# Projection units woven into the index scores and dealt out anew over HGRN; attention blocks in the order 4, 5, 6, 7, 3, 2, 1, 0; a shorter search step; one level mask on ScalarE

## The chip, the cores and the metric

The kernel is one launch on one NeuronCore of one Trainium2 chip. The metric is the device time in microseconds. Its engines run side by side, each in its own order, and wait for each other on semaphores: TensorE (PE, matmuls and transposes into the eight banks of PSUM), VectorE (DVE), ScalarE (ACT), GpSimd (POOL) and SyncE (SP, which issues the weight loads).

## The reference, cut to what matters

One layer of a decoder is computed for a prompt of 1024 tokens and for 8 single tokens ("samples") with a paged cache of 8192 past positions each: an FFN, a mixer, a second FFN, each with a residual and a LayerNorm. All is float32. Only the mixer is touched. It projects the hidden state into everything that the two halves of the mixer need, and then:

```python
# attention half: an indexer scores all keys, the best 256 are attended
logits = einsum('bqhd,bld->bqhl', qi, kidx) * (64 ** -0.5)
score  = einsum('bqh,bqhl->bql', wi * (8 ** -0.5), relu(logits))   # masked causally
_, idx = top_k(score, 256)
o_attn = softmax(q . k[idx]) @ v[idx]                              # 8 heads, 2 kv heads
# HGRN2 half: gated linear recurrence, 8 heads of 64x64 state
f = lb + (1 - lb) * sigmoid(rf);  k = 1 - f
S_t = diag(f_t) S_{t-1} + k_t i_t^T;  o_t = S_t^T q_t
o_r = rmsnorm(o) * norm_g * silu(rg)
m = concat([o_attn, o_r]) @ w_out
```

For prompt positions below 256 every causal key is selected, so the first two blocks of 128 queries (0 and 1) need no search.

## The kernel before, in words

The mixer runs in stages. The prompt is cut into 8 blocks of 128 queries; block b has 128(b+1) keys, so blocks 2 to 7 have widths 384 to 1024. Projections are cut into **units** (`UNITS`): eight matmuls over the model dimension into one PSUM bank, then one ScalarE copy out of it. A long unit ("f", line 528) gives 128 features for 344 tokens, a short one ("t", line 533) 256 or 72 features for 128 tokens. `unit_done` counts finished units, `unit_out` copied ones; unit u uses bank u % 3 and waits until unit u - 3 has been copied.

1. **Units 0 to N1 - 1**: index queries, keys, values, index keys and weights.
2. **Index scores** (PE lines 559 to 576, ACT 918 to 925, DVE 1107 to 1118): for blocks 2 to 7 and each pair of heads TensorE forms both heads' logits, the head with the first 64 rows of the array and the second with the others. ScalarE writes ReLU of one head into one of two buffers, VectorE adds it, times the query's weight, to the block's score. A head's logits fill two banks; a pair uses banks 0 to 3 or 4 to 7 in turn and waits for the ReLUs of the pair before the last. Before all this TensorE waits for `sn_ready`, the score of each sample's new token (five small VectorE operations, lines 1087 to 1092).
3. **32 rounds**: each searches one bit of the 256th largest score of every query on VectorE and ScalarE (32 rounds for 32 bits of a float), while TensorE transposes gathered cache keys of the samples (line 584), runs **one unit** (q, the gates of t = 0, ri), and forms the samples' index logits (line 593).
4. **HGRN** for t = 0 to 3, two heads each, in the level form of a scan: for levels lv = 0 to 7, VectorE forms the operands of a level (`level`, 1272 to 1277), TensorE its products in two halves (`level_products`, 652), and the entries that belong to this level are kept from PSUM in `AT`: by VectorE with a mask for levels 0 to 6 minus one (`mask`, 1286 and 1290: levels 0 to 5), by ScalarE with block copies for levels 6 and 7 (`block_copy`, 952). Units are listed beside the levels (`BESIDE`) and after levels 5 and 6 (`AFTER`). Where a level has two or more, the first runs before the second `count` of the level, else the only one runs after it. Woven in, twice per level, is one step of the samples' own search: `sample_bit` (1160, 1131 to 1133), `sample_compare` (1155, 1156) on VectorE, `count` (607) on TensorE. In t = 1 and 2, VectorE also turns the scores of blocks 7 and 6 into masks (`keep_top`, two parts, in levels 2 and 3). In t = 3 the samples' selection runs instead (`select_a` to `select_d`); its buffers lie over ring slots 0 and 1, so `select_a` waits until all units are out.
5. **Attention** in 64 steps (block, head), blocks 7 down to 0: logits (723), masked maximum on VectorE (1375), exponent on ScalarE (977), transposes (736), copy (987), times values (749). From step 32 on it runs two steps ahead instead of one. `keep_top` of the block two below stands after heads 4 and 5. A sample state update (1393 to 1400) stands after head 6 of the second to fifth block.
6. The output projection (858), LayerNorm, second FFN.

SyncE loads weight slabs into four ring slots in one order. The slab of w_out in slot 2 (`mix(14)`) waits until all six masks are made, since masks are built in that slot.

`link(...)` makes VectorE wait for the end of an instruction before its next one. `NBITS` and `ROUNDS` are 32, `FIRST_TOPK` 2, `H` 8, `BLK` 8, `DT` 8, `TW` 344.

Of the kernel before, what the change touches and what calls it, by code (L numbers as in the profile page):

```python
# [9 lines left out]
def build_decoder_step(nc, I, O):  # L10
# [34 lines left out]
    with ctx:  # L45
# [283 lines left out]
        UNITS += gate_units(0, 0) + gate_units(0, 1) + row_units("ri", 0) + ri1[:5]  # L329
# [24 lines left out]
        assert N2 - N1 == ROUNDS  # L354
# [3 lines left out]

        def steps():

            return [(b, h) for b in range(BLK - 1, -1, -1) for h in range(H)]
# [150 lines left out]
        def pe_mixer(pe, cols, mean, var):  # L512
# [3 lines left out]
            def unit(u):  # L516
                kind, name, m, a, x, _ = UNITS[u]
                pe.wait_ge(ring_in[m % 4], mix_reach[m])
                if kind == "f":
                    pe.wait_ge(ln_done, x + 1)  # L520
                else:
                    pe.wait_ge(ln_done, 2 if x < 5 else 3)
                if u >= 3:
                    pe.wait_ge(unit_out, u - 2)
                for k in range(DT):
                    if kind == "f":
                        w = RING[:, m % 4, :].rearrange("p (k c) -> p k c", c=SLAB)
                        last = M(PS[:, u % 3, 0:TW], w[:, k, P * a:P * a + P], ACTS[:, k, cols(x)],  # L528
                                 start=k == 0, stop=k == DT - 1)
                    else:  # L530
                        rows = P if x < BLK else NB
                        w = RING[:, m % 4, 0:DT * a].rearrange("p (k c) -> p k c", c=a)
                        last = M(PS[0:rows, u % 3, 0:a], ACTS[:, k, P * x:P * x + rows], w[:, k, :],  # L533
                                 start=k == 0, stop=k == DT - 1)
                last.then_inc(unit_done, 1)
# [1758 lines left out]
```

## Time and profile before

| | us |
|---|---|
| median of 3 runs (lowest, highest) | 2722.03 (2721.08, 2722.7) |
| the profiled execution's own time | 2723.82 |
| its span | 2722.1 |
| TensorE busy | 2587.1 (95%) |
| VectorE busy | 1528.5 (56%) |
| ScalarE busy | 664.2 (24%) |
| GpSimd busy | 536.2 (20%) |

Busy times are of single engines in one profiled execution. The chain that ended last gives 80% of the span to PE and 13% to DVE. A matmul's end is modelled, so a busy TensorE is not one at its peak. The granted TensorE clock of a stretch is given as a share of full speed.

### The profile page before, as it was taken

The page shows a single profiled execution, that of the slowest core. Times are in us where ns is not written, and L with a number is a line of the kernel's source. Part 1 is how long each engine was busy: PE and PEld are TensorE (multiplying, and loading weights), DVE is VectorE, ACT ScalarE, POOL GpSimd, SP SyncE. Part 2 cuts the span into 40 slices and gives each one's busy share as a digit, 9 for nine tenths or more (in the row PEclk, how much of TensorE's full clock was granted, in tenths as well). Part 3 has the DMA queues.
Part 4 walks back from the last instruction along what each step waited for, and adds up shares of the span by engine and source line. Part 5 has one row for each costly group of instructions (what it writes and reads, how often), then busy time and mean ns, then how long its engine had stood idle before and what let it go on. Part 6 is the DMA issues. An engine that isn't in the chain of part 4 may idle for free.

```text
span 2722.1 us, 42485 instructions
## 1 busy us (share of the span) xinstructions
PE 2587.1 (95%) x16989; PEld 2360.9 (87%) x16989; DVE 1528.5 (56%) x3030; ACT 664.2 (24%) x1519; POOL 536.2 (20%) x518
## 2 busy tenths in 40 slices
PE   8999999999999979998998789999999999999997
PEld 8989999999998747897766667768999999999997
DVE  5544465546542187797778866425654465546543
ACT  1110122012201255662221156502220022002212
POOL 5230233023301011110000012313330233023300
PEclk9999999999999999999999799999999999999999
DMA  7455246534642113320010012103464346434642
GB/s 187 124 146 137 75 125 170 137 81 124 167 134 77 48 36 93 102 86 1 2 32 1 2 50 66 28 1 93 126 171 129 86 124 167 128 93 124 167 117 90
DMA packets 456371, 261.67 MB, mean 96 GB/s; under 512 B 21720, under 2 KB 448840, under 8 KB 456176
## 3 DMA queue, kind: packets, MB, share of 16 engines
q1 hardware_dynamic: 448736, 238.48, 33.3%
q0 software_dynamic: 7440, 20.49, 2.6%
q8 instruction: 136, 2.23, 0.3%
q14 instruction: 59, 0.48, 0.1%
HBM read 252.12 MB, written 6.81 MB: 95 GB/s over the span
## 4 chain that ended last, share of the span: by engine, by line
PE 80%; DVE 13%; issue 4%; ACT 1%; SPq 1%; DMA 1%; DVEq 0%; ACTq 0%
PE ps L1681 33%; PE ps L1747 20%; PE ps L528 8%; PE ps L533 5%; PE ps L858 4%; PE ps L593 2%; PE ps L652 1%; PE ps L749 1%; DVE down_weights L1118 1%; PE ps L723 1%; PE ps L584 1%; DVE aux L1290 1%; PE ps L736 1%; DMA weight_ring<-ffn_wu 1%; DVE weight_ring L1375 1%
## 5 line engine op out<-in xcount | busy, mean ns | idle before, releaser
L1681 PE MATMUL ps<-aux,big 128*128 128x172 f32 x2112 | 333.5, 311 | 14.7 <-ACT big L1882 14.6
L2062 DVE TENSOR_TENSOR weight_ring<-ps,big 128x172 f32<-128x172 f32 x396 | 123.7, 331 | 386.3 <-ACT big L1882 350.7
L1681 PEld LDWEIGHTS ps<-aux,big 128*128 128x128 f32 x2112 | 315.8, 191 | 19.9 <-ACT big L1882 17.9
L1681 PE MATMUL ps<-acts,weight_ring 128*128 128x172 f32 x2112 | 322.9, 311 | 9.7 <-DMA weight_ring<-ffn_wg 5.3
L1681 PE MATMUL ps<-weight_ring 128*128 128x172 f32 x2112 | 329.5, 309 | 0.0
L1681 PEld LDWEIGHTS ps<-acts,weight_ring 128*128 128x128 f32 x2112 | 314.0, 192 | 11.6 <-DMA weight_ring<-ffn_wg 5.6
L1681 PEld LDWEIGHTS ps<-weight_ring 128*128 128x128 f32 x2112 | 313.8, 190 | 0.0
L1747 PE MATMUL ps<-big 128*128 128x172 f32 x1584 | 238.8, 309 | 0.0
L1747 PEld LDWEIGHTS ps<-big 128*128 128x128 f32 x1584 | 233.1, 190 | 0.0
L528 PE MATMUL ps<-acts,weight_ring 128*128 128x344 f32 x768 | 230.8, 456 | 0.0
L2222 POOL TENSOR_TENSOR big<-weight_ring 128x512 f32<-128x512 f32 x66 | 83.7, 1269 | 666.3 <-PE ps L1681 619.8
L1882 ACT ACTIVATE big<-ps 128x172 f32<-128x172 f32 x396 | 117.6, 309 | 390.5 <-PE ps L1681 390.5
L528 PEld LDWEIGHTS ps<-acts,weight_ring 128*128 128x128 f32 x768 | 144.3, 191 | 71.8 <-issue 2.0
L1886 ACT ACTIVATE weight_ring<-weight_ring 128x172 f32<-128x172 f32 x198 | 68.0, 343 | 487.1 <-DVE weight_ring L2062 487.1
L533 PE MATMUL ps<-weight_ring,acts 128*128 128x256 f32 (+3 forms) x864 | 179.1, 362 | 0.0
L2123 DVE SCALAR_TENSOR_TENSOR acts<-acts,ps 128x172 f32<-128x172 f32 x96 | 31.7, 331 | 251.4 <-PE ps L1747 251.4
L1681 PE MATMUL ps<-acts,big 128*128 128x172 f32 x1056 | 165.6, 310 | 0.0
L533 PEld LDWEIGHTS ps<-weight_ring,acts 128*128 128x128 f32 (+1 forms) x864 | 141.9, 179 | 26.6 <-issue 1.3
L1747 PE MATMUL ps<-big,weight_ring 128*128 128x172 f32 x1056 | 159.9, 309 | 0.0
L1747 PE MATMUL ps<-big,down_weights 128*128 128x172 f32 x1056 | 159.9, 309 | 0.0
L1681 PEld LDWEIGHTS ps<-acts,big 128*128 128x128 f32 x1056 | 158.1, 191 | 0.0
L1747 PEld LDWEIGHTS ps<-big,down_weights 128*128 128x128 f32 x1056 | 155.5, 190 | 0.0
(344 smaller groups left out, 3676.7 us busy)
## 6 DMA issues: line engine op xcount, KB each, us to landing
weight_ring<-ffn_wg SPq DMA_DIRECT2D x132, 512.0 KB, 5.2
weight_ring<-ffn_wu SPq DMA_DIRECT2D x132, 512.0 KB, 7.1
down_weights<-ffn_wd SPq DMA_DIRECT2D x24, 1408.0 KB, 11.6
weight_ring<-ffn_wd SPq DMA_DIRECT2D x24, 1408.0 KB, 9.5
weight_ring<-w_in SPq DMA_DIRECT2D x9, 1024.0 KB, 5.2
weight_ring<-w_in SPq DMA_DIRECT2D x8, 512.0 KB, 5.2
weight_ring<-w_out SPq DMA_DIRECT2D x4, 1024.0 KB, 6.2
big<-x_prompt SPq DMA_DIRECT2D x7, 512.0 KB, 6.1
```

Source lines behind the costliest of these rows:

```text
L528: last = M(PS[:, u % 3, 0:TW], w[:, k, P * a:P * a + P], ACTS[:, k, cols(x)], start=k == 0, stop=k == DT - 1)
L533: last = M(PS[0:rows, u % 3, 0:a], ACTS[:, k, P * x:P * x + rows], w[:, k, :], start=k == 0, stop=k == DT - 1)
L584: last = T(PS[:, 3 + j // 4, P * (j % 4):P * (j % 4) + P], KX[:, r % 4, P * j:P * j + P], IDENT[:, :])
L593: last = M(PS[:, 5 + r % 2, 32 * j:32 * j + 32], KXT[:, r % 2, P * j:P * j + P], QB[:, :, :, 2 * gp:2 * gp + 2], start=True, stop=True)
L858: last = M(PS[:, Y_BANK[y], 0:TW], w[:, k, P * (d % 2):P * (d % 2) + P], src, start=k == 0, stop=k == DT - 1)
L1681: last = M(PS[:, 3 * m + bank, 0:QW], lhs[:, i, :], rhs[:, i, :], start=begin and i == 0, stop=end and i == KH - 1, skip_group_check=True)
L1747: last = M(PS[:, x + bank, 0:QW], lhs[:, i, :], rhs[:, i, :], start=begin and i == 0, stop=end and i == LAST, skip_group_check=True)
L1882: A(ST[:, m, c, :], PS[:, 3 * m, 0:QW], ACT.Copy).then_inc(cp_done, 1)
L1886: A(CG[:, i, :], CG[:, i, :], ACT.Silu).then_inc(sl_done, 1)
L2062: V.tensor_tensor((CG, CU)[m][:, (out, i)[m], :], PS[:, 3 * m + bank, 0:QW], ST[:, m, part, :], ALU.add)\
L2123: V.scalar_tensor_tensor(a, a, 2 * ALPHA, PS[:, x + bank, 0:QW], ALU.mult, ALU.add).then_inc(zr_done, 1)
L2222: G.tensor_tensor(s1, a21, a22, ALU.add).then_inc(su_done[0], 1)
```

## The change

Four long units (q) are taken out of the rounds: one stands before the index scores, in place of the wait for the new tokens' scores, three are cut into single k steps, one after each pair of heads. To free banks 0 and 1 for them, scores use banks 2 to 7 as three slots instead of four, with another wait. All nine units of ri, second half, then lie in the rounds, and the rest is dealt out anew over HGRN. Level 5's mask goes to ScalarE. The attention order becomes 4, 5, 6, 7, 3, 2, 1, 0, with the masks one block ahead and only block 4's within HGRN. The samples' search step is rewritten.

```diff
+        WOVEN = 4
+        def unit_bank(u):
+            return (u - N1) % 2 if N1 <= u < N1 + WOVEN else u % 3
+        def bank_free(u):
+            return u if u == N1 + WOVEN else u - 1 if N1 + 2 <= u < N1 + WOVEN else u - 2
...
-        UNITS += gate_units(0, 0) + gate_units(0, 1) + row_units("ri", 0) + ri1[:5]
+        UNITS += gate_units(0, 0) + gate_units(0, 1) + row_units("ri", 0) + ri1
...
-        for beside, spread in (([g1[0], *rg0[:2], g1[1], *rg0[2:4], g1[2], *rg0[4:6]], (2, 1, 2, 1, 2, 1, 0, 0)),
-                               ([g2[0], *rg0[6:8], g2[1], rg0[8], ri1[5], g2[2], *ri1[6:]], (2, 1, 2, 1, 2, 2, 0, 0)),
-                               ([g3[0], *rg1[:2], g3[1], *rg1[2:4], g3[2], *rg1[4:6]], (2, 1, 2, 1, 2, 1, 0, 0)),
-                               (rg1[6:], (2, 1, 0, 0, 0, 0, 0, 0))):
+        for beside, spread in (([g1[0], *rg0[:2], g1[1], *rg0[2:4], g1[2], rg0[4]], (2, 1, 2, 1, 1, 1, 0, 0)),
+                               ([g2[0], *rg0[5:7], g2[1], *rg0[7:9], g2[2], rg1[0]], (2, 1, 2, 1, 1, 1, 0, 0)),
+                               ([g3[0], rg1[1], g3[1], rg1[2], g3[2], rg1[3]], (1, 1, 1, 1, 1, 1, 0, 0)),
+                               (rg1[4:], (2, 2, 1, 0, 0, 0, 0, 0))):
...
+        ORDER = (4, 5, 6, 7, 3, 2, 1, 0)
...
+            unit(N1)
-            pe.wait_ge(k3_ready, 9)
-            pe.wait_ge(sn_ready, 1)
+            pe.wait_ge(k3_ready, 10)
...
-                if pr >= 2:
-                    pe.wait_ge(ix_relu, 2 * pr - 2)
+                if pr:
+                    pe.wait_ge(ix_relu, 2 * pr - 1)
...
-                        last = M(PS[:, 4 * (pr % 2) + 2 * e + c // 512, 0:min(512, n - c)], QIT[rows, hp, P * b:P * b + P],
+                        last = M(PS[:, 2 + 2 * ((2 * pr + e) % 3) + c // 512, 0:min(512, n - c)], QIT[rows, hp, P * b:P * b + P],
...
+                unit(N1 + 1 + pr // DT, pr % DT, pr % DT + 1)
...
-                unit(N1 + r)
+                unit(N1 + WOVEN + r)
...
-                    if lv >= 6:
+                    if lv >= 5:
                         block_copy(t, lv)
...
+            def new_scores():
+                dve.wait_ge(k3_ready, 10)
+                link(V.tensor_tensor(QIPROD, QITOK, KIW[0:NB, 8:9, 0:HD].to_broadcast([NB, H, HD]), ALU.mult))
...
                 if h == 0:
+                    if i == H:
+                        new_scores()
...
                 link(V.tensor_tensor(DCMP, SDEC, cand[:, 6:10].unsqueeze(2).to_broadcast([P, 4, PAGE + 1]), ALU.is_ge))
+                V.tensor_scalar(CAND[:, 6:10], CAND[:, 6:10], BITS[:, k + 1:k + 2], None, ALU.bitwise_xor)
                 V.tensor_reduce(DCNT, DCMP, AX.X, ALU.add).then_inc(dcmp_done, 1)
...
-                next_bit(slice(6, 10), k)
+                link(V.scalar_tensor_tensor(CAND[:, 6:10], REJ[:, 6:10], BITS[:, k:k + 1], CAND[:, 6:10],
+                                            ALU.bitwise_and, ALU.bitwise_xor))
...
-                    if lv < 7:
+                    if lv < 6:
                         mask(t, lv - 1)
                     sample_slot(t, lv, 1)
-                    if 0 < t < 3 and lv in (2, 3):
-                        keep_top(BLK - t, lv - 2)
+                    if t == 2 and lv in (2, 3):
+                        keep_top(ORDER[0], lv - 2)
...
-                if i % H in (4, 5) and STEPS[i][0] - 2 >= FIRST_TOPK:
-                    keep_top(STEPS[i][0] - 2, i % H - 4)
+                if i % H in (4, 5) and i // H < 7 and ORDER[i // H + 1] >= FIRST_TOPK:
+                    keep_top(ORDER[i // H + 1], i % H - 4)
...
-                        if t == 1:
+                        if t == 2:
                             mix(14)
```

The three woven units run to the last pair of heads, eight k steps each; ScalarE copies each out after 16 ReLUs. At the start of the kernel one of the small mask-building steps on VectorE moves to an earlier place. The waits on counts of masks and copies are renumbered to match.

## Rows read from the trace of the kernel before

**Rows 1.** Windows, all engines: us, busy us of each engine (x instructions), PEclk, DMA.

```profile
966.82:1016.60 49.78, 36.84 (x161) 14.62 (x161) 42.65 (x47) 36.22 (x48) 8.74 (x16) 0.94 0.15 27
1238.28:1313.10 74.82, 70.12 (x439) 55.85 (x439) 58.16 (x107) 11.59 (x18) 0.95 (x1) 0.95 0.00 1
1324.39:1407.47 83.08, 75.18 (x454) 57.10 (x455) 67.63 (x120) 14.71 (x23) 1.50 (x1) 0.92 0.10 27
1418.69:1497.11 78.42, 69.01 (x436) 53.95 (x437) 64.79 (x114) 15.64 (x23) 1.50 (x1) 0.96 0.00 1
1508.32:1528.57 20.25, 19.20 (x160) 15.39 (x160) 16.53 (x23) 5.20 (x8) 0.00 (x0) 0.92 0.01 2
1577.26:1746.75 169.49, 155.77 (x1144) 122.76 (x1145) 98.98 (x270) 101.45 (x216) 52.11 (x54) 0.97 0.22 57
```

**Rows 2.** Lines by form, index scores: busy us, mean ns, idle before.

```profile
L1118 DVE SCALAR_TENSOR_TENSOR down_weights<-big,aux,down_weights 128x1024 f32<-128x1024 f32 x7 | 9.0, 1284 | 0.8 <-ACT big L925 0.2
...
L1118 DVE SCALAR_TENSOR_TENSOR down_weights<-big,aux,down_weights 128x384 f32<-128x384 f32 x7 | 4.3, 618 | 0.8
...
L925 ACT ACTIVATE big<-ps 128x1024 f32<-128x1024 f32 x8 | 8.2, 1024 | 2.5 <-DVE down_weights L1118 2.5
...
L925 ACT ACTIVATE big<-ps 128x384 f32<-128x384 f32 x8 | 3.8, 491 | 7.6 <-PE ps L572 7.2 <-DVE down_weights L1118 0.4
```

**Rows 3.** Timeline, start of the index scores: start us, us, engine, line, operation [idle before].

```profile
966.82 6.76 PE L572 MATMUL ps<-big 64*128 64x384 f32 x20 [2.80 <-issue]
```

**Rows 4.** Timeline, attention, a pair of 1024-wide logits and its reader.

```profile
1592.88 1.99 PE L723 MATMUL ps<-big 64*128 64x512 f32 x8
...
1594.89 1.23 DVE L1375 CUSTOM_DVE_ANT_0 weight_ring<-ps,down_weights 128x1024 f32<-128x1024 f32 x1 [3.96 <-PE ps L723]
```

**Rows 5.** Chain that ended last, a long and a short round: start us, us.

```profile
1041.10 4.63 PE ps L528 x16
...
1161.83 3.46 PE ps L533 x16
```

**Rows 6.** Timeline of VectorE, HGRN t = 0.

```profile
1236.35 0.17 DVE L1251 COPY down_weights<-big 128x8 f32<-128x8 f32 x1
...
1236.43 0.69 DVE L1252 TENSOR_SCALAR big<-big 128x1032 f32<-128x1032 f32 x1
...
1263.26 0.16 DVE L1160 TENSOR_SCALAR rejected<-ps 128x4 int32<-128x4 f32 x1 [2.13 <-PE ps L607]
...
1264.18 0.70 DVE L1155 TENSOR_TENSOR big<-down_weights,candidate 128x516 bf16<-128x516 f32 x1
...
1265.52 2.47 DVE L1290 COPY_PREDICATED aux<-level_masks,ps 128x1024 f32<-128x1024 uint8 x2
...
1267.89 0.14 DVE L1160 TENSOR_SCALAR rejected<-ps 128x4 int32<-128x4 f32 x1
...
1270.13 0.68 DVE L1272 TENSOR_TENSOR weight_ring<-big,weight_ring 128x512 f32<-128x512 f32 x1
...
1272.78 0.16 DVE L1160 TENSOR_SCALAR rejected<-ps 128x4 int32<-128x4 f32 x1
```

**Rows 7.** Timeline of TensorE, HGRN t = 0.

```profile
1276.47 3.65 PE L652 MATMUL ps<-weight_ring 64*128 64x128 f32 x32 [0.90 <-DVE aux L1290]
...
1303.55 9.50 PE L528 MATMUL ps<-acts,weight_ring 128*128 128x344 f32 x32
```

**Rows 8.** Timeline of ScalarE, level-6 block copies of t = 0.

```profile
1302.01 1.65 ACT L952 ACTIVATE aux<-ps 32x256 f32<-32x256 f32 x4 [5.46 <-PE ps L652]
```

**Rows 9.** Windows of VectorE over keep_top: 1024 first, 640 first, 1024 second.

```profile
1344.29:1348.91 4.62, 4.48 (x6) 1.00 0.02 4
1625.44:1628.66 3.22, 3.08 (x6) 1.00 0.14 41
...
1358.43:1361.79 3.36, 3.26 (x4) 1.00 0.00 0
```

**Rows 10.** Timeline of TensorE, attention, logits behind the 640-wide mask.

```profile
1630.00 1.77 PE L723 MATMUL ps<-big 64*128 64x512 f32 x8 [1.04 <-DVE small L1377]
```

More of the change, by code:

```diff
@@ L353, in build_decoder_step @@
         ROUNDS = 32
-        assert N2 - N1 == ROUNDS
+        assert N2 - N1 - WOVEN == ROUNDS
         DEC_SLOTS = [(t, lv, e) for t in range(3) for lv in range(2, 8) for e in range(2) if lv < 7 or e == 0][:NBITS]
+        ORDER = (4, 5, 6, 7, 3, 2, 1, 0)
+        MASKED_AT = {b: n + 1 for n, b in enumerate(b for b in ORDER if b >= FIRST_TOPK)}
         def steps():
-            return [(b, h) for b in range(BLK - 1, -1, -1) for h in range(H)]
+            return [(b, h) for b in ORDER for h in range(H)]
         STEPS = steps()
@@ L514, in pe_mixer, with unit @@
             loaded = [0]
-            def unit(u):
+            def unit(u, first=0, end=DT):
                 kind, name, m, a, x, _ = UNITS[u]
[L518 to L525, printed above, removed]
+                if first == 0:
+                    pe.wait_ge(ring_in[m % 4], mix_reach[m])
+                    pe.wait_ge(ln_done, x + 1 if kind == "f" else 2 if x < 5 else 3)
+                    if u >= 3:
+                        pe.wait_ge(unit_out, bank_free(u))
+                for k in range(first, end):
                     if kind == "f":
                         w = RING[:, m % 4, :].rearrange("p (k c) -> p k c", c=SLAB)
-                        last = M(PS[:, u % 3, 0:TW], w[:, k, P * a:P * a + P], ACTS[:, k, cols(x)],
+                        last = M(PS[:, unit_bank(u), 0:TW], w[:, k, P * a:P * a + P], ACTS[:, k, cols(x)],
                                  start=k == 0, stop=k == DT - 1)
@@ L532, in unit @@
                         w = RING[:, m % 4, 0:DT * a].rearrange("p (k c) -> p k c", c=a)
-                        last = M(PS[0:rows, u % 3, 0:a], ACTS[:, k, P * x:P * x + rows], w[:, k, :],
+                        last = M(PS[0:rows, unit_bank(u), 0:a], ACTS[:, k, P * x:P * x + rows], w[:, k, :],
                                  start=k == 0, stop=k == DT - 1)
-                last.then_inc(unit_done, 1)
+                if end == DT:
+                    last.then_inc(unit_done, 1)
             def turn_heads(b):
@@ L640, in level_products @@
                 for half in range(2):
-                    if 1 <= lv <= 6:
-                        pe.wait_ge(h_at, 12 * t + 2 * (lv - 1) + half + 1)
-                    elif lv == 7:
-                        pe.wait_ge(h_ax, 4 * t + half + 1)
+                    if 1 <= lv <= 5:
+                        pe.wait_ge(h_at, 10 * t + 2 * (lv - 1) + half + 1)
+                    elif lv >= 6:
+                        pe.wait_ge(h_ax, 6 * t + 2 * (lv - 6) + half + 1)
                     elif t and half:
@@ L684, in pe_mixer @@
                 last.then_inc(h_kt_mm, 1)
-                pe.wait_ge(h_at, 12 * (t + 1))
-                pe.wait_ge(h_ax, 4 * (t + 1))
+                pe.wait_ge(h_at, 10 * (t + 1))
+                pe.wait_ge(h_ax, 6 * (t + 1))
                 def out(hd, c):
@@ L758, in turn_gated @@
             def turn_gated(bi):
-                b = BLK - 1 - bi
+                b = ORDER[bi]
                 if bi < 7:
@@ L882, in unit @@
                 width = TW if kind == "f" else a
-                src = PS[0:rows, u % 3, 0:width]
+                src = PS[0:rows, unit_bank(u), 0:width]
                 cols = slice(TW * x, TW * x + TW)
@@ L917, in act_mixer @@
             A(WIS[0:NB, BLK, :], KIW[0:NB, BLK, HD:HD + H], ACT.Copy, scale=H ** -0.5).then_inc(wis_ready, 1)
+            unit(N1)
             for i in range(6 * H):
@@ L922, in act_mixer @@
                     act.wait_ge(ix_acc, i - 1)
-                k0 = 4 * (i // 2 % 2) + 2 * (i % 2)
+                k0 = 2 + 2 * (i % 3)
                 src = PS[:, k0:k0 + 2, :].rearrange("p u c -> p (u c)")[:, 0:n]
                 A(RELU[:, i % 2, 0:n], src, ACT.Relu, scale=KSCALE).then_inc(ix_relu, 1)
+                if i % 16 == 15:
+                    unit(N1 + 1 + i // 16)
             def keys_out(r):
@@ L941, in act_mixer @@
                 pass_counts(r)
-                unit(N1 + r)
+                unit(N1 + WOVEN + r)
             def block_copy(t, lv):
@@ L989, in out_rows @@
             def out_rows(bi):
-                b = BLK - 1 - bi
+                b = ORDER[bi]
                 act.wait_ge(at_ott, bi + 1)
@@ L1288, in mask @@
                         m = LEVELS[:, lv - 1, :].unsqueeze(1).unsqueeze(1).to_broadcast([P, 2, 4, P])
-                        dve.wait_ge(h_at, 12 * t + 2 * (lv - 1) + half + 1)
+                        dve.wait_ge(h_at, 10 * t + 2 * (lv - 1) + half + 1)
                         V.copy_predicated(at, m, ps).then_inc(h_at, 1)
@@ L2147, in ffn @@
                         if ff == 0 and g == 0:
-                            if 1 <= j <= 7:
-                                dve_consts(dve, V, link, j - 1)
+                            if j == 1:
+                                dve_consts(dve, V, link, 0)
+                            if 1 <= j <= 6:
+                                dve_consts(dve, V, link, j)
                             if 1 <= j <= 6:
```

19 lines of the change are left out of this document (9 added, 10 removed).

## The prediction

> **What bounds the kernel now.** I read the stages first (stretches cut at matmul starts), then in each stage the order of instructions, and there which wait ends last. TensorE is busy almost everywhere, but not for one reason. In the index scores [rows 1] it is busy 36.8 of 49.8 us: VectorE, 42.7 busy, sets the pace, and ScalarE (36.2) must refill a two-deep buffer. In the search rounds TensorE runs without a gap. In HGRN, units t = 0, 1, 2 take 74.8, 83.1 and 78.4 us from the first to the eighth group of level products, TensorE busy 70.1, 75.2 and 69.0 [rows 1]: it waits for VectorE in the middle levels and VectorE waits for it at the rest. Attention has 155.8 busy of 169.5. Nothing in the two FFNs or the output projection is touched, so only these stages count.
>
> **1. Four projection units into the index scores, and the waits there.** One unit (eight k steps, 4.63 us [rows 5]) now stands ahead of the scores, in place of the 2.80 us that TensorE idled for the new token's score [rows 3]. The idle began at 964.0; the unit ends near 968.6, so the first score pair starts 1.8 us later than 966.82. What follows is the part against the change. Before, a pair wrote into four slots and waited for the ReLU of the pair before the last one; now there are three slots and the wait is for the first ReLU of the *previous* pair. That closes a ring: pair, its first ReLU, next pair. At 1024 keys the pair needs 2.01 us until a waiting engine can start (1592.88 to 1594.89, same matmuls [rows 4]), ReLU 1.02 [rows 2], and 0.06 taken for TensorE's restart (an estimate; the reader in [rows 4] started 0.02 after the modelled end): 3.09 us. VectorE needs 2 x 1.39 = 2.78 for the two heads (1.284, and 0.8 idle in seven [rows 2]). At 384 keys: a matmul column costs 4630/8/344 = 1.68 ns, so 2.01 - 640 x 0.00168 = 0.94, with ReLU 0.49 and 0.06 it is 1.49, against 2 x 0.73 = 1.46. Linear between, the mean ring is 2.29 us; 24 pairs give 55.0, and the last ReLU 1.0: 56.0 where 49.8 stand. Sum: 1.8 + 56.0 - 49.8 = **+8.0**. The k step of 0.58 us per pair hides behind the ReLU (at 384 keys, 0.49, it just doesn't). The new token's score, moved behind the first block (some 2 us on VectorE, part of the 2.80 that TensorE waited for it [rows 3]), falls into VectorE's new slack. Ends: +3 if the ring doesn't bind (start 1.8, the moved score 2.0, less a first pair that is no longer at the low clock), +11 if it binds and each k step adds 0.13.
> A page of the Trainium skill, "Perfetto Trace Analysis" (Optimization Strategy), says that the same gap repeating on the engine that should be busy can mean too little PSUM for the next tile. By that rule a slot taken from the scores costs, as the ring says; before's rows show no such gap on VectorE.
>
> **2. Rounds.** Each round is gapless on TensorE, and unit forms differ: 4.63 against 3.46 us [rows 5]. The 32 rounds held 18 long units and 14 short, now 14 and 18: 4 x 1.17 = **-4.7**. Should VectorE be the tighter one in a short round, the gain is less: 3 at the lower end, an estimate.
>
> **3. HGRN.** Edits with one answer: fewer units beside the levels, the level-5 mask to ScalarE, the top-k masks out of t = 1, a short search step. Prices on VectorE [rows 6]: search step 0.92 (1263.26 to 1264.18), compare 1.34, mask 2.37, level operands 2.65 (1270.13 to 1272.78). The step loses two operations of about 0.26 and 0.20 (and + xor become one, taken at 0.26) and its last xor stands unlinked in the compare; the nearest row is a small operation that lets the next start after 0.08 (1236.35 to 1236.43 [rows 6]). New pair of step and compare: 0.46 + 1.42 = 1.88 for 2.26, 0.38 less. Bounds: 0.20 (xor costs 0.26) to 0.46.
> The Trainium skill, "VectorE: DVE Perf Modes" (The DRAIN you can't avoid), says the next operation doesn't start until the pipe is empty, whatever the semaphores. By it the unlinked xor costs full price and the step saves 0.20; the sum would be 2 us less. The 0.08 row speaks for the larger saving.
> Level by level with these prices, TensorE's units 4.73 and 3.55 from start to start, products 2.0, two more units in a row 9.50 [rows 7]:
> t = 0. Nothing moves until the third products. Then masks 2, 3 come 0.4 and 1.2 us earlier. In level 4 the lone long unit now stands *behind* the count, so VectorE no longer waits for it: mask 4 starts 4.8 us earlier. From there TensorE is the bound: short unit, long, products, two long; the level-5 mask on ScalarE (eight small copies, at most 0.41 each by the wider ones [rows 8], 3.3 us) is hidden behind 8.3 us of units. Eighth products at 1307.6 instead of 1313.1: -5.5.
> t = 1. Also loses the 1024-wide mask, 4.62 and 3.36 us [rows 9], and one unit more from level 5. Same ladder: 68.7 from first to eighth products where 83.1 stand: -14.4.
> t = 2. Units (1,1,1,1,1,1) instead of (2,1,2,1,2,1), and a 640-wide mask (3.22 [rows 9], its second part in the same proportion 2.35) for the 896-wide one (between the two, about 4.15 and 3.0). TensorE idles 2.7 us at level 3, VectorE's work sets levels 2 to 5, then units again: 68.2 for 78.4: -10.2.
> t = 3. Five short units instead of three, in levels 0, 1, 2. The sample selection waits until all units have left the banks it reuses. Before, it started 20.25 us after the first products [rows 1]; now products 3.6, two units 7.1, products 2.0, two units 7.1, products 2.0, one unit and its copy 4.0 give 25.8: +5.6. Later its chain is VectorE's without a gap, and loses the mask: -2.4. Together +3.2.
> These sum to -26.9. Against it stands the clock. After idling TensorE runs a product group in 3.65 us instead of 2.06 (at 1276.47, with 0.90 idle right ahead [rows 7]). With fewer units there is about one more such group in each of t = 0, 1, 2, and half of its 1.6 us reaches the path: +2.4. HGRN: **-24.5**, bounds -29 and -15.
>
> **4. Attention in the order 4, 5, 6, 7, 3, ...** The first block is 640 wide instead of 1024: its logits, maximum and exponent, all serial at the start, shrink by 384 columns at 3.36 ns (TensorE, half clock), 1.04 and 0.83 ns ((1284 - 618)/640 and (1024 - 491)/640 [rows 2]): 1.3, 0.4 and 0.3, and a wait two heads later by an estimated 0.6: -2.6. But the masks now prepared are 768, 896, 1024, 512 and 384 wide, in blocks of width 640, 768, 896, 1024 and 512. Before, the 640 mask in the 896 block held the next logits back by 1.04 us [rows 10]. A 1024 mask there puts 4.62 for 3.22: 1.4 more, and the second part (3.36 for 2.35) delays the next wait, behind the sample state, by 1.0. The 768 block with an 896 mask pays the same 2.4; the first block 0.4 net (its second wait has no sample state ahead); block 7 wins 0.9; block 3, which had no mask, pays 1.2. Sum of stalls +5.5, attention **+2.9**, bounds -1 and +9. The w_out load that waits for the last mask comes one block later and still over 30 us ahead of its use: nothing.
>
> **Sum.** +8.0 - 4.7 - 24.5 + 2.9 = -18.3. The profiled execution took 2723.8 (span 2722.1 and 1.7 around it), the runs' median is 2722.0; the difference is applied to the median: 2703.7 us.
>
> **Rivals.**
> A, the ring doesn't bind: semaphore latency overlaps the pair's tail, or the pair is faster than the attention row. Index scores +3, all else the same: 2698.7. For it: with slots four deep no row shows the ring. Against: each of its terms is a row. Chance 0.20.
> B, small blocks can't hide big masks: the steps after a mask queue behind each other, so that each of the three wide masks stalls TensorE by its full second part too (2.7, 3.0, 3.4, less the 1.0 counted): +8 in attention: 2712. For it: the blocks are narrower where the masks are wider. Against: the 1.04 [rows 10] was a third of its mask. Chance 0.15.
> C, slower: the clock of HGRN. If TensorE, with its filler thinned, stays at 1.2 GHz through levels 2 to 5 of t = 0, 1, 2, four product groups (1.6 each), two long (4.7) and two short units (3.5) per t grow by 22.8 us, of which some 8 fall into waits: 45 in three, net +27: 2749. It decides from 6 us per t on. For it: the selection part of t = 3 and the group at 1276.47 ran so. Against: granted clock was 0.92 to 0.96 in t = 0, 1, 2 [rows 1], and a unit right behind each slow group ran at full speed. Chance 0.05.
> The Trainium skill, "TensorE: Matmul & The Clock Gate" (HAM oscillation), warns of this: matmul bursts split by waits run at half clock again and again. The selection part of t = 3 agrees; the rest, at 0.92 and above, doesn't so far.
>
> **How the numbers follow.** Forecast 0.60, A 0.20, B 0.15, C 0.05. Forecast's own range: HGRN and attention bounds combined, 2695 to 2712. The range reaches to A less 7 and B plus 4: 2692 to 2716; C lies outside. What a measurement tells from no change is 0.2%, 5.4 us, so up to 2716.6 is faster: faster 0.93, within 0.02, slower 0.05.
>
> **What would show it.** Index scores: 56 us between first score pair and first key transpose, TensorE waiting on ScalarE's ReLU in each pair, VectorE with gaps of 0.3 at 1024 keys (right), or VectorE gapless (A). Rounds: 14 at 7.24 and 18 at 6.07. First to eighth products: 69.3, 68.7, 68.2 us plus slow groups; selection 25.8 after t = 3's first products. Attention: 172 us with stalls ahead of the logits at the fifth head of blocks 4, 5, 6. Wrong if the ladders miss by over 5 us in one t, or if a granted clock below 0.9 appears there.

## The result, and the profile after

The changed kernel takes 2701.62 us, median of 4 runs (2697.87 to 2704.78), against 2722.36 before on the same chip: ratio 0.9926, 95% interval 0.9912 to 0.994. A second series gave 2700.54 (8 runs, 2698.4 to 2717.56) against 2722.31: 0.9931, interval 0.9913 to 0.9949. The forecast of 2703.7 lies 2 us off, but that is partly luck: the stages show four errors, one of them of 10 us, that cancel in part and leave 5. The profiled execution took 2700.48 us, its span is 2698.8 where 2722.1 stood: 23.3 less, where the sum said 18.3.

Stages are cut at the start of their first TensorE instruction, in us:

| stage | before | after | difference | forecast |
|---|---|---|---|---|
| first FFN | 856.33 | 846.38 | -9.95 | 0 |
| units up to the one ahead of the scores | 107.1 | 107.1 | 0 | 0 |
| index scores, with the start and the unit ahead | 53.2 | 63.0 | +9.8 | +8.0 |
| rounds | 221.68 | 215.23 | -6.45 | -4.7 |
| HGRN | 338.98 | 314.65 | -24.3 | -24.5 |
| attention | 169.49 | 177.17 | +7.7 | +2.9 |
| output projection, second FFN | 975.35 | 975.32 | 0 | 0 |

The windows of the profile after, columns as in [rows 1]: scores, rounds, and the three HGRN parts t = 0, 1, 2 from first to eighth products, then t = 3 up to attention, attention, and its first 10 us.

```profile
958.64:1016.43 57.79, 53.00 (x210) 20.57 (x209) 44.01 (x52) 35.48 (x52) 7.72 (x14) 1.00 0.12 24
1016.43:1231.66 215.23, 211.32 (x1281) 177.73 (x1281) 188.20 (x524) 134.90 (x258) 29.45 (x30) 0.99 0.30 94
...
1231.66:1302.35 70.69, 68.21 (x422) 53.45 (x422) 53.30 (x96) 13.34 (x25) 0.95 (x1) 0.92 0.00 1
1313.65:1383.07 69.42, 66.33 (x423) 50.47 (x423) 54.50 (x99) 17.38 (x30) 1.50 (x1) 0.95 0.06 17
1394.29:1462.79 68.50, 62.29 (x389) 47.49 (x390) 58.07 (x102) 16.62 (x28) 1.50 (x1) 0.90 0.01 1
1474.00:1546.31 72.31, 53.28 (x477) 46.19 (x477) 58.85 (x125) 16.09 (x30) 1.84 (x3) 0.81 0.01 2
1546.31:1723.48 177.17, 160.50 (x1144) 126.06 (x1145) 108.40 (x278) 101.22 (x216) 52.15 (x54) 0.94 0.21 55
1546.31:1556.31 10.00, 7.97 (x30) 5.13 (x31) 6.33 (x18) 3.69 (x7) 3.06 (x3) 0.50 0.73 209
```

In [rows 1] the same stages had TensorE busy 36.84, 70.12, 75.18, 69.01 and 155.77. Attention is the stage to look at: its length grew by 7.7, but TensorE's idle time only from 13.7 to 16.7 (length less busy). The other 4.7 us are the same work done slower, at a granted clock of 0.94 for 0.97.

**Index scores.** The timeline of TensorE in the changed kernel, at 512 and at 1024 keys (L581 the pair, L536 the woven k step):

```profile
968.02 0.85 PE L536 MATMUL ps<-acts,weight_ring 128*128 128x344 f32 x2
970.00 1.13 PE L581 MATMUL ps<-big 64*128 64x512 f32 x4 [1.14 <-ACT big L936]
...
1006.23 1.99 PE L581 MATMUL ps<-big 64*128 64x512 f32 x8 [0.33 <-ACT big L936]
1008.15 0.85 PE L536 MATMUL ps<-acts,weight_ring 128*128 128x344 f32 x2
1009.32 1.99 PE L581 MATMUL ps<-big 64*128 64x512 f32 x8 [0.33 <-ACT big L936]
```

From pair to pair it is 3.09 us at 1024 keys, as forecast, and TensorE waits 0.33 for ScalarE's ReLU each time. Ahead of 970.00 it waits 1.14 longer: there VectorE forms the new tokens' scores, which the forecast let fall into slack.

**First FFN.** What the forecast never looked at. SyncE's load queue (SPq; ffn_wd is the down-projection's weights, ffn_wg and ffn_wu the up-projections') and TensorE in the kernel before:

```profile
163.48 3.71 SPq L1560 DMA_DIRECT2D down_weights<-ffn_wd  x2
167.23 6.60 SPq L1543 DMA_DIRECT2D weight_ring<-ffn_wg  x2
173.87 3.68 SPq L1543 DMA_DIRECT2D weight_ring<-ffn_wu  x2
...
179.55 2.66 PE L1681 MATMUL ps<-acts,weight_ring 128*128 128x172 f32 x8 [5.33 <-DMA weight_ring<-ffn_wg]
183.16 5.92 PE L1681 MATMUL ps<-acts,weight_ring 128*128 128x172 f32 x24 [0.94 <-DMA weight_ring<-ffn_wu]
```

And in the changed kernel, where TensorE has no stall at that place:

```profile
147.24 0.16 DVE L1071 TENSOR_TENSOR lower_bound<-lower_bound 128x4 f32<-128x4 f32 x1
...
147.69 3.73 SPq L1580 DMA_DIRECT2D down_weights<-ffn_wd  x2
157.04 1.13 SPq L1563 DMA_DIRECT2D weight_ring<-ffn_wg  x2
158.22 4.78 SPq L1563 DMA_DIRECT2D weight_ring<-ffn_wu  x2
```

The first down-projection load waits, on SyncE, for `lb_diff`: a VectorE operation that ends the last of the small mask-building steps. The change moved six of these steps, not one, as the section on the change has it: steps 1 to 6 each stand one pair of features earlier, the last one at the sixth instead of the seventh. The load starts 15.8 us earlier, and so do the up-projection loads that queue behind it.

### The profile page after: what moved, and what is told of

Read it like the earlier page. It is cut to its first block, busy times and chain, and to the rows that moved or that the text cites. A ratio compares the mean times of both kernels' runs of the same rounds, so it can differ in the third digit from the quotient of the medians.

```text
span 2698.8 us, 42468 instructions
## 1 busy us (share of the span) xinstructions
PE 2592.4 (96%) x16989; PEld 2357.3 (87%) x16989; DVE 1510.3 (56%) x2990; ACT 670.5 (25%) x1552; POOL 536.1 (20%) x518
## 4 chain that ended last, share of the span: by engine, by line
PE 83%; DVE 11%; issue 3%; ACT 2%; SPq 1%; DMA 0%; DVEq 0%; ACTq 0%
PE ps L1701 33%; PE ps L1767 20%; PE ps L536 8%; PE ps L541 6%; PE ps L868 4%; PE ps L603 2%; PE ps L759 2%; PE ps L662 1%; PE ps L733 1%; PE ps L581 1%; PE ps L594 1%; PE ps L746 1%; DVE aux L1310 1%; DVE weight_ring L1395 1%; SPq L1563 1%
## 5 line engine op out<-in xcount | busy, mean ns | idle before, releaser
L536 PE MATMUL ps<-acts,weight_ring 128*128 128x344 f32 x768 | 240.8, 465 | 0.0
L536 PEld LDWEIGHTS ps<-acts,weight_ring 128*128 128x128 f32 x768 | 145.1, 195 | 80.7 <-issue 16.4
```

What stands on the lines that cost most here:

```text
L536: last = M(PS[:, unit_bank(u), 0:TW], w[:, k, P * a:P * a + P], ACTS[:, k, cols(x)], start=k == 0, stop=k == DT - 1)
```

## Experiments

Medians are of runs beside runs of the kernel before on the same chip, unless a stage is named; stage lengths come from the profile of each kernel.

**1 and 2. The load that waits for a mask-building step.** The same edit put into the kernel before, and taken out of the changed one:

```diff
-                            if 1 <= j <= 7:
-                                dve_consts(dve, V, link, j - 1)
+                            if j == 1:
+                                dve_consts(dve, V, link, 0)
+                            if 1 <= j <= 6:
+                                dve_consts(dve, V, link, j)
```

> The kernel before, with only the order of the small mask-building steps in the first FFN taken from the changed kernel: step 6, which ends in the difference of the lower bounds that the first down-projection load waits for, stands behind the sixth pair of features instead of the seventh. Theory (SyncE's in-order queue stood at that load, and the loads of the up weights queued behind it came too late): the load is issued near 147.7 us instead of 163.5, TensorE's stall of 5.33 us at 179.55 and the slow matmuls behind it are gone, the first mixer unit starts near 846.4 instead of 856.3, and the time falls by 10 us to 2712. Rival (the late weights are of another origin, such as where the buffers lie or what else the DMA engines carry): the stall at 179.55 stays and the time is within 2 us of the kernel before.

> The changed kernel with only that order put back as it was before. Theory: the stall of 5.3 us near 179.6 returns, the first mixer unit starts near 856, and the time is 2711.5, 10 us above the changed kernel. Rival: no stall returns, and the time stays at 2701 to 2703.

Before with the edit: 2714.3 (2710.62 to 2716.27), ratio 0.997, interval 0.9959 to 0.9982; first FFN 846.26 us for 856.33, all other stages within 0.4. The changed kernel without it: 2710.99 (2708.79 to 2712.2), ratio 0.9958, interval 0.9942 to 0.9975; first FFN 857.97. Its timeline has the late load and the stall again:

```profile
162.99 3.46 SPq L1580 DMA_DIRECT2D down_weights<-ffn_wd  x2
...
180.32 2.66 PE L1701 MATMUL ps<-acts,weight_ring 128*128 128x172 f32 x8 [6.58 <-DMA weight_ring<-ffn_wg]
```

Both ways: six small steps on VectorE, one pair of features earlier, are worth 8.0 us beside the kernel before and 10.45 beside the changed kernel (2700.54 in the same series), between 0.37 and 0.48 of the whole gain of 21.8. The stall itself is 5.33 + 0.94; the rest is that the matmuls behind it ran 8 in 2.66 and 24 in 5.92 us, where the same kind runs 32 in 4.83 (the mean granted clock from 171.72 to 191.00 us was 0.73).

**3. The changed kernel again.** No edit.

> The changed kernel once more, unaltered, to see what lies behind the 7 us between its runs. If it is TensorE's clock in the attention part, this profile has another granted clock than 0.94 there and the attention part another length than 177.2 us, at the same stalls; if it is the HGRN part, the groups of level products at half speed differ in number (first to eighth products were 70.7, 69.4, 68.5). FFNs, units, scores and rounds should repeat within 0.5 us each.

HGRN took 311.78 us (70.0, 68.0, 67.6 in t = 0, 1, 2) for 314.65 (70.7, 69.4, 68.5), at the same instructions: the granted clocks were 0.94, 0.97 and 0.95 for 0.92, 0.95 and 0.90. Attention repeated to 0.01 us, the first FFN came out 2.5 longer, at a granted clock of 0.95 between 40 and 60 us where the first profile had 1.00. So attention did not differ between these two profiles; in experiments 2, 4, 5, 8 and 9, with the same code there, it does. The FFN was expected to repeat within 0.5 us and did not; half clock from 58.0 to 61.4 us is worth at most 1.7 of the 2.5 us, and the rest stays open. The run of 2717.56 us has no profile, but its granted clock over the whole execution was 0.976, where the other seven had 0.980 to 0.984; in which stage it lost the time stays open.

**4. Each head waits for its own slot.** In the scores:

```diff
-                if pr:
-                    pe.wait_ge(ix_relu, 2 * pr - 1)
...
                     for e in range(2):
+                        if pr and c == 0 and 2 * pr - 2 + e > 0:
+                            pe.wait_ge(ix_relu, 2 * pr - 2 + e)
```

> The changed kernel, but in the index scores each head's matmuls wait only for the ReLU that frees their own slot (head i for head i-3), instead of both heads of a pair for the later one. The first chunk of a pair's first head can then run during the previous pair's ReLU. Theory (the ring pair, first ReLU, next pair sets 3.09 us at 1024 keys): the pair's period falls to what TensorE itself has to do, pair 1.99 and slice 0.77, 2.8 us at 1024 keys, 2.55 at 896, 2.33 at 768, unchanged below; the index scores take 2.5 to 3 us less than 62.95. Rival (TensorE's own time or VectorE's adding sets the pace already, the ring only looks like it): no change within 0.5 us.

Scores 56.03 us for 57.79: 1.8 saved, where 2.5 to 3 were expected. The pairs start without a gap now, but alternate in length:

```profile
1002.51 1.99 PE L581 MATMUL ps<-big 64*128 64x512 f32 x8
1004.43 0.84 PE L536 MATMUL ps<-acts,weight_ring 128*128 128x344 f32 x2
1005.21 2.38 PE L581 MATMUL ps<-big 64*128 64x512 f32 x8
```

Two pairs take 5.78 us, 2.89 each for 3.09; forecast 2.8. The wait was the ring's. In every other pair the first head's chunk runs alone while the second waits (their first matmuls start 0.40 us apart), and TensorE spends 0.39 us more. The time (2705.33, 2699.55 to 2711.5) shows nothing of the 1.8 us. In this profile attention had 179.27 us at a granted clock of 0.93, and HGRN 317.24, 2.6 and 5.5 more than in the two profiles of the changed kernel. The mean clock of HGRN is not lower (0.91 for 0.91 and 0.93), but its half-clock stretches fall elsewhere: from the first to the second group of products of t = 2 TensorE never idles and needs 9.72 us at 0.68 instead of 7.14 at 1.00, and in t = 1 13.11 us at 0.77 instead of 11.98 at 0.86 and 10.60 at 1.00. Experiment 11, with the same scores, repeats both (13.13 and 9.74, HGRN 317.26), so the saving in the scores may be paid for in HGRN; what ties the two is not shown.

**5. All units ahead of the scores.**

```diff
-            unit(N1)
+            for u in range(N1, N1 + WOVEN):
+                unit(u)
...
-                unit(N1 + 1 + pr // DT, pr % DT, pr % DT + 1)
```

> The changed kernel with all four units ahead of the index scores, none of their k steps between the pairs; the three slots and their waits stay. Theory of the ring: the pair's period at 1024 keys stays 3.09 us and at 384 keys falls from 1.62 to the ring's 1.49; the mean over the six widths is 2.29, so 24 pairs and the last ReLU take 56.0, and the three units add 13.9 ahead. Rival (the k steps are what lengthens the pairs): 1024 keys fall to VectorE's 2.78.

The copies on ScalarE moved with the units. The timeline of TensorE at 384, 640 and 1024 keys:

```profile
974.14 0.92 PE L582 MATMUL ps<-big 64*128 64x384 f32 x4 [0.57 <-ACT big L937]
975.63 0.92 PE L582 MATMUL ps<-big 64*128 64x384 f32 x4 [0.57 <-ACT big L937]
...
991.65 2.51 PE L582 MATMUL ps<-big 64*128 64x512 f32 x8 [0.79 <-ACT big L937]
994.94 2.51 PE L582 MATMUL ps<-big 64*128 64x512 f32 x8 [0.79 <-ACT big L937]
...
1030.00 1.99 PE L582 MATMUL ps<-big 64*128 64x512 f32 x8 [1.11 <-ACT big L937]
1033.10 1.99 PE L582 MATMUL ps<-big 64*128 64x512 f32 x8 [1.11 <-ACT big L937]
```

1.49 and 3.09 us a pair at the two ends: the forecast's ring to the hundredth. With the k steps it was 1.62 and 3.09, so they are hidden at 1024 keys and cost 0.13 a pair at 384. They do a second thing: without them TensorE idles 0.57 to 0.68 in every pair and falls to half clock from 985.60 to 1005; pairs at 640 keys then need 2.51 us instead of 1.35 and the period is 3.29 for 2.14. The scores took 64.46, not 56.0, and the kernel 2732.59 (2719.39 to 2741.91; the profile is of the fastest of these eight runs).

**6. Falling order of the blocks.**

```diff
-        ORDER = (4, 5, 6, 7, 3, 2, 1, 0)
+        ORDER = (7, 6, 5, 4, 3, 2, 1, 0)
```

> The changed kernel with the attention blocks in falling order 7, 6, 5, 4, 3, 2, 1, 0; the masks still stand one block ahead, so only block 7's lies within HGRN (t = 2). Each mask is then 128 keys narrower than the block that it stands in, not 128 wider. Theory (the added stalls come from masks wider than their block): start 1.7 us later (1024 keys), stalls behind the first mask part down from 2.4 to about 1.4 each, attention 174 to 175 us for 177.2; t = 2 of HGRN 1 to 3 us longer by the 1024-wide mask. Rival (the stall comes from the place of the mask behind the fifth head, whatever its width): attention stays at 177 to 179.

Attention 175.65 us. The start is 2.0 longer (6.54 from the first logits to the first transposes, for 4.53), the three stalls of 2.25, 2.37 and 2.44 ahead of the logits are gone, eight of 0.8 to 1.6 us stand ahead of logits instead of one, and TensorE's clock is full from 20 us on. t = 2 of HGRN 70.0 for 67.6 to 68.5. Median of two runs 2694.94 (2694.84 and 2695.04), 0.9902 of before (0.9882 to 0.9922). In sum TensorE idled more than in rising order, 18.9 us for 16.7, but was busy for 156.75 instead of 160.50:

```profile
1543.82:1719.47 175.65, 156.75 (x1145) 122.11 (x1145) 105.89 (x278) 101.11 (x216) 52.62 (x54) 0.96 0.22 55
```

The rising order does save waiting, and gives more than that back in clock; its stalls are fewer but longer. That their length is what lowers the clock is not shown. The expectation of 174 to 175 us was missed by 0.65, the rival's 177 to 179 by more. Of the 5.7 us between the two profiles (2693.1 for 2698.8) attention has only 1.5, HGRN 2.2, and the part behind attention, where nothing differs, 1.6 (973.6 for 975.3).

**7. The mask behind the fourth head.**

```diff
-                if i % H in (4, 5) and i // H < 7 and ORDER[i // H + 1] >= FIRST_TOPK:
-                    keep_top(ORDER[i // H + 1], i % H - 4)
+                if i % H in (3, 5) and i // H < 7 and ORDER[i // H + 1] >= FIRST_TOPK:
+                    keep_top(ORDER[i // H + 1], (i % H - 3) // 2)
```

> The changed kernel with the first part of each mask made in attention moved from behind the fifth head of the block to behind the fourth; the second part stays behind the sixth. Logits are formed for two heads at a time and only after the even head's transposes, so behind an even head VectorE's queue is what TensorE waits for next, behind an odd head TensorE has a pair of logits (1.77 us), two heads' products and one set of transposes ahead. Theory: the stalls of 2.25, 2.37 and 2.44 us ahead of the logits go or fall below 0.8, and with them the matmuls at low clock right behind them; attention 171 to 173 us for 177.2, the time 4 to 6 us below the changed kernel. Rival (VectorE's work per block is too much wherever it stands): the stalls reappear ahead of the transposes of the next head at the same size, attention within 1 us of 177.2.

Attention 172.75 us, 12.1 of them idle for 16.7. The three long stalls ahead of the logits went, four of 1.2 to 1.7 us came ahead of the transposes instead, so only half of what was expected of the stalls is right:

```profile
1561.94 1.23 PE L746 MATMUL ps<-ident,weight_ring 128*128 128x128 f32 x5 [1.23 <-ACT weight_ring L1000]
1586.39 0.84 PE L746 MATMUL ps<-ident,weight_ring 128*128 128x128 f32 x6 [1.55 <-ACT weight_ring L1000]
```

The whole gain is waiting: TensorE was busy for 160.63 us as before (160.50), at the same granted clock of 0.94, so the matmuls at low clock did not go with the stalls. Median 2698.13 (2692.86 to 2702.19), 0.9918 of before (0.9902 to 0.9935), which overlaps with the changed kernel's interval.

**8. Level 5 back on VectorE.** `block_copy` from level 6, `mask` up to level 5, and the counts of waits with them.

> The changed kernel with the entries of level 5 kept by VectorE with a mask again, in all four t. Theory of the forecast's ladder: 2.37 us more on VectorE in level 6; TensorE is the bound there in t = 0 and 1, so these grow by 0.5 to 2 us each, t = 2 by 2.4 and t = 3 by 2.4 (its chain is VectorE's). HGRN 6 to 8 us longer than 311.8 to 314.7. Rival (the eight small copies on ScalarE cost as much as the mask saves): HGRN within 1.5 us.

t = 0, 1, 2: 69.82, 68.04, 67.62, the same to 0.03 us as in experiment 7's profile, whose HGRN is the changed kernel's; t = 3 74.61 for 72.3. So the move is worth 2.3 us, all in t = 3, and the expectation of 6 to 8 us for HGRN missed: the 2.4 of t = 2 and the 0.5 to 2 of t = 0 and 1 are not there. (In nine profiles with the changed kernel's code in t = 3 that part took 70.9 to 72.4 us, so the price is good to about 1.5.) The kernel took 2709.25 (2703.56 to 2710.57), and 8 us of it are in attention, where nothing was changed: 185.09 us. Same stall, same code, timeline of TensorE first in this kernel:

```profile
1565.90 2.50 PE L733 MATMUL ps<-big 64*128 64x512 f32 x8 [2.25 <-DVE small L1397]
1568.33 2.39 PE L759 MATMUL ps<-big,weight_ring 128*128 128x64 f32 x10
1570.52 1.27 PE L746 MATMUL ps<-ident,weight_ring 128*128 128x128 f32 x5
```

and in the changed kernel:

```profile
1565.09 1.35 PE L733 MATMUL ps<-big 64*128 64x512 f32 x8 [2.25 <-DVE small L1397]
1566.37 1.33 PE L759 MATMUL ps<-big,weight_ring 128*128 128x64 f32 x10
1567.54 0.72 PE L746 MATMUL ps<-ident,weight_ring 128*128 128x128 f32 x5
```

The stalls are equal to the hundredth; what stands behind them runs at 1.2 or at 2.4 GHz. Here it stayed at or near 1.2 for the two windows that follow (columns as before):

```profile
1567.14:1577.14 10.00, 10.00 (x44) 7.79 (x42) 3.22 (x8) 3.50 (x7) 2.10 (x2) 0.50 0.05 13
1577.14:1587.14 10.00, 10.00 (x48) 7.91 (x44) 2.64 (x7) 3.57 (x6) 1.99 (x2) 0.56 0.05 13
```

**9. The long search step.**

```diff
-                V.tensor_scalar(CAND[:, 6:10], CAND[:, 6:10], BITS[:, k + 1:k + 2], None, ALU.bitwise_xor)
...
-                link(V.scalar_tensor_tensor(CAND[:, 6:10], REJ[:, 6:10], BITS[:, k:k + 1], CAND[:, 6:10],
-                                            ALU.bitwise_and, ALU.bitwise_xor))
+                next_bit(slice(6, 10), k)
```

> The changed kernel with the samples' search step as before: two more linked small operations on four values per step, no xor inside the compare. Theory: 0.38 us per step and compare on VectorE; the steps of levels 2 to 5 lie on the path in t = 2 (8 x 0.38 = 3.0), half of them in t = 0 and 1 (1.5 each), none at level 6 and 7: HGRN +5 to +7. Rival 1: the steps wait for TensorE's count anyway, HGRN within 1 us. Rival 2: the unlinked xor costs its full 0.26 and the saving is 0.20 a pair, HGRN +3; the spacing of the small operations in the two traces shows which.

HGRN 319.71 us, 5.1 and 7.9 more than in the changed kernel's two profiles, for an expected 5 to 7: t = 0, 1, 2 at 73.02, 71.60, 70.47, each 2.0 to 3.6 above. The saving lies in all three alike, not mainly in t = 2. VectorE in the changed kernel, one step and compare:

```profile
1261.07 0.15 DVE L1179 TENSOR_SCALAR rejected<-ps 128x4 int32<-128x4 f32 x1
1261.25 0.22 DVE L1180 SCALAR_TENSOR_TENSOR candidate<-rejected,bits,candidate 128x4 uint32<-128x4 uint32 x1
1261.51 0.70 DVE L1173 TENSOR_TENSOR big<-down_weights,candidate 128x516 bf16<-128x516 f32 x1
1262.24 0.23 DVE L1174 TENSOR_SCALAR candidate<-candidate,bits 128x4 uint32<-128x4 uint32 x1
1262.38 0.68 DVE L1175 TENSOR_REDUCE small<-big 128x4 f32<-128x516 bf16 x1
1262.98 0.68 DVE L1292 TENSOR_TENSOR weight_ring<-big,weight_ring 128x512 f32<-128x512 f32 x1
```

and with the long step, first and last of the group:

```profile
1265.28 0.15 DVE L1178 TENSOR_SCALAR rejected<-ps 128x4 int32<-128x4 f32 x1
...
1267.53 0.68 DVE L1290 TENSOR_TENSOR weight_ring<-big,weight_ring 128x512 f32<-128x512 f32 x1
```

1.91 for 2.25: 0.34 saved, forecast 0.38 with bounds 0.20 and 0.46. The unlinked xor costs 0.14 (1262.24 to 1262.38), where a linked one costs 0.26. Attention stood at 183.76 us here, again by the clock; median 2711.56 (2708.74 to 2715.3).

**10. The two VectorE edits alone.** The short step and level 5 on ScalarE, in the kernel before.

> The kernel before with two edits of HGRN alone: the short search step, and level 5's entries kept by ScalarE. Units, scores, masks of the prompt and the order of the blocks as before. Undone one at a time in the changed kernel they cost 5 to 8 us and 2.3 us. Theory (the gain of 24 to 27 in HGRN is theirs for some 10, and the rest belongs to the units and to the wide mask taken from t = 1): HGRN 339.0 falls by 9 to 12, t = 1 stays above 78. Rival (in the old order VectorE is ahead of TensorE, so the two edits are worth little until the units are dealt out anew): less than 5.

HGRN 329.63 for 338.98: -9.35. t = 0 to 2 at 73.38, 80.50 and 75.71 (-1.4, -2.6, -2.7 from [rows 1]), and -2.6 in t = 3. So of the 24 to 27 us, 9.4 are those edits', as expected, and by subtraction the remaining 15 to 18 belong to the units dealt out anew and the masks taken out or narrowed, t = 1 first. The two groups were not separated further. Median 2715.88 (2714.16 to 2716.45), 0.9974 of before (0.9964 to 0.9984).

**11 and 12. Both mends together**, experiments 4 and 7 in one, in rising and in falling order.

> The changed kernel with both mends: in the scores each head waits only for its own slot, and the first part of each mask in attention stands behind the fourth head of the block. They lie in different parts, so they should add: scores 56.0, attention 172.7 (TensorE's clock at full speed from 30 us into it), a median of 2695 to 2697, 4 to 6 us below the changed kernel.

> The same two mends, and the blocks in falling order 7 to 0. Attention had 175.65 us in falling order with stalls of 0.8 to 1.6 us at four places; with the first mask part behind the fourth head they go: 171 to 173. t = 2 of HGRN 70.0 for 67.6. Median 2690 to 2693, and runs that differ by less than 4 us, since no stall of over 1.3 us is left behind the first 15 us of attention. Rival (the order doesn't matter once the mask stands right): within 1.5 us of the rising version.

Rising: 2695.46 (2690.36 to 2701.14), 0.9894 of before (0.9877 to 0.9911). Falling: 2693.84 (2692.17 to 2694.29), 0.9895 (0.9878 to 0.9911). Both end below the changed kernel's intervals; between the two the medians don't decide: the falling version is 0.8 above its expectation, and 1.6 from the rising one, where the rival said at most 1.5. The four runs of the rising version spread over 11 us, those of the falling one over 2. Scores were 56.03 in both. Attention had 172.18 in falling order; in rising order 177.99 instead of the 172.7 expected, with 166.40 busy where experiment 7 had 160.63: the same code again, at a mean clock of 0.91 for 0.94. The falling version has a stall of 1.70 us left at 126 us into the stage, which was to be gone. In falling order t = 2 took 71.43, 1.4 over the expectation.

## Why the prediction was right, and where it was wrong

**"Nothing in the two FFNs or the output projection is touched": wrong, 9.95 us.** The largest error of the forecast. The diff does touch the first FFN, in one place; who waits for the end of the last of the moved steps was not asked. The profile of before had the answer, the 5.33 us of TensorE waiting for a DMA. Experiments 1 and 2 show cause and size from both sides.

**Index scores: the ring was right, its surroundings were not.** The start came 1.8 us later, as forecast. The period is 3.09 and, alone, 1.49; the mend of experiment 4 removes the wait, so rival A is out. The scores took 57.8 where the sum had 56.0. Terms mis-sized: the k step costs 0.77 us of TensorE, not 0.58, and shows at 384 keys with 0.13 a pair; the new tokens' scores stall TensorE by 1.14 since they stand in the ring, where VectorE's slack of 0.3 a pair only comes at wide blocks. So of the 2.80 that TensorE had waited for them [rows 3], 1.14 came back.

**Rounds: -6.45 for -4.7.** The unit forms explain 4.7. The other 1.7 is the first round, which in the kernel before ran at half clock after 3.56 us of waiting for the last ReLU: from its first key transposes to those of the second round 8.95 us, now 7.26.

```profile
1016.60 1.63 PE L584 MATMUL ps<-ident,weight_ring 128*128 128x128 f32 x8 [3.56 <-ACT big L925]
1018.02 5.99 PE L528 MATMUL ps<-acts,weight_ring 128*128 128x344 f32 x16
```

and in the changed kernel:

```profile
1016.43 1.09 PE L594 MATMUL ps<-ident,weight_ring 128*128 128x128 f32 x8 [1.25 <-ACT big L936]
1017.36 4.79 PE L536 MATMUL ps<-acts,weight_ring 128*128 128x344 f32 x16
```

The long unit of [rows 5] shows its length at full clock, 4.63. The woven slices keep TensorE busier to the end of the scores (53.00 of 57.79 us, 36.84 of 49.78 before), and the term was left out.

**HGRN: -24.3 for -24.5, and in a second profile -27.2.** The ladders of 69.3, 68.7 and 68.2 us met 70.7, 69.4, 68.5 and 70.0, 68.0, 67.6. The selection started 25.98 us after t = 3's first products (1474.00 to 1499.98), forecast 25.8, and t = 3 grew by 3.4 for 3.2. Two expectations drawn from it later put a price in the wrong place: level 5's mask was to save in t = 0, 1 and 2 as well and saves 2.3 us in t = 3 alone (experiment 8), and the short step saves 2 to 3.6 us in each of t = 0, 1, 2 instead of mostly in t = 2 (experiment 9). The forecast's view that TensorE is the bound from level 4 on in t = 0 and 1 was thus too strong. Rival C didn't occur: the granted clock was 0.90 to 0.97 in both profiles of the changed kernel, though 0.88 in t = 2 with the scores of experiment 4.

**Attention: +7.7 for +2.9.** The forecast's +2.9 is 4.2 us more waiting and 1.3 less matmul time, since it took 1.3 of its 2.6 at the start from the logits. Measured, TensorE's idle time grew by 2.95 (13.72 to 16.67) and its busy time by 4.73. That 2.95 is near 2.9 is chance. The waits, in the timeline of the changed kernel:

```profile
1570.35 0.74 PE L746 MATMUL ps<-ident,weight_ring 128*128 128x128 f32 x5 [1.04 <-ACT weight_ring L1000]
1589.78 1.84 PE L733 MATMUL ps<-big 64*128 64x512 f32 x8 [2.37 <-DVE small L1397]
...
1621.94 3.30 PE L733 MATMUL ps<-big 64*128 64x512 f32 x8 [2.44 <-DVE small L1397]
```

The stall behind the first part of a wide mask was priced at 1.04 + 1.4 = 2.44 in blocks 5 and 6 and measured 2.37 and 2.44 (2.25 in block 4). The second part, priced at 1.0 more in each of blocks 5 and 6, makes TensorE wait 1.04 us in block 4 and nowhere 0.3 us or more in blocks 5 and 6. Rival B had the full second part as a wait in all three, so it is out. The term that was off is the matmul time, which the forecast had at -1.3: +4.7 us in this profile, +12.8 in that of experiment 8 (168.58 busy for [rows 1]'s 155.77). Not all of it stands behind the wide masks: the first 10 us of the stage ran at 0.50, where the kernel before had 0.68. Experiment 6 (waiting +2.2, matmuls -3.75) acts through the clock; experiment 7 (waiting -4.6, matmuls +0.1) acts through the wait alone. The forecast weighed the clock in HGRN, whose mean hardly moved (0.91 before and after), and left it out in attention. The warning of the Trainium skill, "TensorE: Matmul & The Clock Gate" (HAM oscillation), that matmul bursts split by waits run at half clock again and again, fits this stage in part: its first 10 us ran at 0.50, and the 10 us around the stalls of 2.37 and 2.44 us at 0.73 and 0.83, but the matmuls behind the 2.25 us stall kept full speed here.

**The sum.** Errors of -9.95, +1.8, -1.75, +0.2 and +4.8 give -4.9 of the 5.0 by which the span's -23.3 misses -18.3. The hit in the total says nothing for the single terms: with the mask-building steps left where they were the changed kernel takes 2710.99 us (experiment 2), 7 above the forecast, though still inside its range of 2692 to 2716.

## What to carry to other kernels

When an edit moves even a 0.2 us operation, list the semaphores that it raises and who waits for them; an in-order load queue turns such a wait into late weights many microseconds on. Price a stall on TensorE as the wait plus what may run at half clock behind it, in every stage, and prefer the place in another engine's queue that has most of TensorE's own work ahead of the next need. Check a sum stage by stage: a total that is right within 2 us held an error of 10.

## What the runs showed of the hardware

The same attention code, with 15.6 to 16.7 us of idle TensorE, took 177.17, 177.18, 179.03, 179.27, 178.95, 183.76 and 185.09 us in seven profiles (the changed kernel twice, and experiments 2, 4, 5, 9, 8); only the granted clock differs, 0.90 to 0.94 on average. Which level follows on a stall of 2.25 us could not be told from the stall. The part behind attention has two lengths as well, whatever stands ahead of it: 973.6 to 974.0 us in seven profiles and 975.3 in the other seven. So a change of under 5 us in such a kernel is read from one stage, its idle and its busy time, and not from the median alone. Less waiting did not mean less spread: of the last two kernels the rising one idles 11.6 us in attention and its four runs lie 11 us apart, the falling one idles 12.6 and its runs lie 2 apart.

An unlinked VectorE operation on four values behind a 516-wide one costs 0.14 us, linked 0.26. The Trainium skill, "VectorE: DVE Perf Modes" (The DRAIN you can't avoid), says that the next operation starts only when the pipe is empty, and that one which is not held starts earlier. The trace agrees with the second half: the reduce behind the xor starts 0.09 before the xor's recorded end (1262.38 for 1262.24 + 0.23).

Small copies on ScalarE: a level-5 copy (16 partitions by 128 elements) has 0.27 us, level 6 (32 by 256) 0.37, level 7 (64 by 512) 0.59; the forecast took at most 0.41 for the first.
